# Product-key expert block: two token blocks by gathered rows and two by plain float32 products, in place of one and three

## The reference, cut to what matters

```python
q = (hf @ w_query).reshape(T, PEER_HEADS, 2, PEER_HALF)
s = jnp.einsum('thpd,pkd->thpk', q, sub_keys).astype(jnp.float32)
sv, si = lax.top_k(s, PEER_TOPK)
cand = (sv[:, :, 0, :, None] + sv[:, :, 1, None, :]).reshape(T, PEER_HEADS, PEER_TOPK * PEER_TOPK)
...
top_s, top_pos = lax.top_k(cand, PEER_TOPK)
idx = jnp.take_along_axis(cand_idx, top_pos, axis=-1)
g = jax.nn.softmax(top_s, axis=-1)
...
u = down[ib]
pre = jnp.einsum('td,thkd->thk', hb, u).astype(jnp.float32)
w = (gb * jax.nn.gelu(pre, approximate=False)).astype(hb.dtype)
return jnp.einsum('thk,thkd->td', w, up[ib])
```

## Time and profile before

| | before |
|---|---|
| median of 3 runs | 2176.43 us (2176.3 to 2180.94) |
| span of the profiled execution | 2176.0 us |
| TensorE busy | 1860.8 us (86%) |
| VectorE busy | 1542.3 us (71%) |
| ScalarE busy | 868.6 us (40%) |
| GpSimd busy | 740.9 us (34%) |
| bytes moved | 462.65 MB, 213 GB/s over the span |

### The profile page before, as it was taken

One profiled execution on the slowest core, in us unless ns is written; L12 is line 12 of the kernel. 1 busy time (PEld: TensorE's weight loads), 2 busy tenths in 40 slices (PEclk: granted clock), 3 DMA queues, 4 the chain that ended last, 5 costly groups with the idle time before them and its releaser, 6 DMA issues.

```text
span 2176.0 us, 27879 instructions
## 1 busy us (share of the span) xinstructions
PE 1860.8 (86%) x9219; PEld 1632.1 (75%) x9219; DVE 1542.3 (71%) x2326; ACT 868.6 (40%) x1434; POOL 740.9 (34%) x410
## 2 busy tenths in 40 slices
PE   2888999877397999979886888878869999999996
PEld 1676887844276889979886888878857888888884
DVE  5476445386756229967889787977857888888886
ACT  2232222355222244356633665355643333333332
POOL 0000000000000016677755777568763333333320
PEclk7898999987698999989987998979979999999998
DMA  7244442100231225578864887568889999999993
GB/s 266 96 144 150 177 153 95 40 1 1 96 107 58 97 72 171 168 241 278 289 217 151 286 285 262 176 215 291 279 310 352 354 359 357 352 352 360 347 360 142
DMA packets 177680, 462.65 MB, mean 213 GB/s; under 512 B 14624, under 2 KB 96800, under 8 KB 165152
## 3 DMA queue, kind: packets, MB, share of 16 engines
q1 hardware_dynamic: 117808, 272.99, 36.4%
q0 software_dynamic: 37872, 137.90, 18.6%
q10 hardware_dynamic: 21888, 50.34, 5.9%
HBM read 406.12 MB, written 55.05 MB: 212 GB/s over the span
## 4 chain that ended last, share of the span: by engine, by line
PE 53%; issue 15%; DVE 14%; POOL 11%; DVEq 3%; DMA 2%; ACT 2%; POOLq 0%; ACTq 0%; SPq 0%
PE bank L538 16%; PE bank L539 16%; PE bank L540 16%; POOL d_ring L1546 7%; POOL dlo L1523 4%; DVEq L1123 1%; DMA raw<-in_ada 1%; DMA d_ring<-in_down,idxd 1%; DVE att_max L1231 1%; DVE acc_ada L1077 1%; DVE onehot L1394 1%; PE bank L605 1%; DVE wlo L1096 1%; PE bank L593 1%; PE bank L724 1%
## 5 line engine op out<-in xcount | busy, mean ns | idle before, releaser
L1523 POOL TENSOR_TENSOR dlo<-draw,dhi 128x1024 fp32r<-128x1024 f32 x131 | 359.8, 2753 | 1002.4 <-ACT dhi L966 1002.0
L538 PE MATMUL bank<-r_hi,dhi 128*128 128x384 f32 x1024 | 360.2, 352 | 10.1 <-issue 5.5
L539 PE MATMUL bank<-r_lo,dhi 128*128 128x384 f32 x1024 | 355.4, 347 | 0.0
L540 PE MATMUL bank<-r_hi,dlo 128*128 128x384 f32 x1024 | 354.6, 346 | 0.0
L538 PE MATMUL bank<-uhi,w_hi 128*128 128x512 f32 x768 | 300.4, 391 | 17.4 <-issue 13.6
L539 PE MATMUL bank<-ulo,w_hi 128*128 128x512 f32 x768 | 299.7, 390 | 0.0
L540 PE MATMUL bank<-uhi,w_lo 128*128 128x512 f32 x768 | 299.7, 390 | 0.0
L1573 POOL DMA_INDIRECT u_ring<-in_up,idxc x128 | 170.6, 1333 | 276.7 <-DVE accum L1485 252.8
L1445 DVE CUSTOM_DVE_ANT_0 dot_junk<-d_ring,h2row 128x1024 f32<-128x1024 f32 x135 | 194.8, 1443 | 93.2 <-DMA d_ring<-in_down,idxd 83.8
L1038 ACT ACTIVATE uhi<-uraw 128x1024 fp32r<-128x1024 f32 x130 | 137.9, 1062 | 294.0 <-PE bank L540 181.6
L1096 DVE TENSOR_TENSOR wlo<-raw,whi 128x2048 fp32r<-128x2048 f32 x45 | 103.2, 2293 | 176.2 <-ACT whi L801 175.8
(11 more groups left out here) (218 smaller groups left out, 3599.0 us busy)
## 6 DMA issues: line engine op xcount, KB each, us to landing
draw<-in_downT SPq DMA_DIRECT2D x131, 512.0 KB
uraw<-in_up SPq DMA_DIRECT2D x130, 512.0 KB, 7.8
raw<-in_ada SPq DMA_DIRECT2D x24, 1024.0 KB, 4.9
ged<-ge ACTq DMA_DIRECT2D x128, 192.0 KB
gmat<-gstage ACTq DMA_DIRECT2D x24, 1024.0 KB, 7.2
gtile<-gmat SPq DMA_DIRECT2D x16, 1536.0 KB
gein<-ged SPq DMA_DIRECT2D x128, 192.0 KB, 7.2
raw<-in_w_query SPq DMA_DIRECT2D x8, 1024.0 KB, 4.9
```

What stands on the lines that cost most here:

```text
L538: pe.matmul(dst, lhi, rhi, start=first, stop=False)
L539: pe.matmul(dst, lhi, rlo, start=False, stop=False)
L540: return pe.matmul(dst, llo, rhi, start=False, stop=last)
L1523: pool.tensor_tensor(dlo[slot][:, :, :].rearrange("p a b -> p (a b)"), draw[:, slot, :], dhi[:, slot].rearrange("p a b -> p (a b)").bitcas ...
```

## The change

- Two blocks (0 and 1) are gathered, two (2 and 3, `DT` = 256 tokens) are dense. 256 gathers of `down` pass a ring of 4 buffers, 256 of `up` a ring of 8, of which four are the same and four lie over `h2T`.
- The dense products are plain float32, with no split: 8 products of 256 columns a tile of `down`, 4 products of 512 columns a tile of `up`. Tiles stream through 4 buffers. No `dhi`, `dlo`, `uhi`, `ulo`, `w_hi`, `w_lo`.
- The GELU results of all 128 tiles stay in SBUF (`wmat`, 128 KB a partition). After the last `down` tile a loop of 64 groups of four tokens builds one-hots (8 small VectorE instructions), multiplies them on TensorE (4 products), and multiplies the result into `wmat` in place (one VectorE instruction, 128x128x4, with a step of 1 KB between groups of 4 numbers in `wmat` and of 512 B between numbers in PSUM). Only then does the `up` half begin. `ged` and `gmat` are gone.
- `route` keeps, of the 256 pair sums, the 72 that can be among the top 16, and turns positions back by a short chain of small instructions (`unpair`). The dot products stand between its instructions (`dots`), one or two at a time, for blocks 1 to 3; 42 follow after the softmax, the other 88 after the 64 groups.
- The token-major copy of the block's vectors (`h2tok`) and the gate row move into the query stage.

The core of the diff:

```diff
-DTB = 3
-DT = DTB * P
+GB = 2
+DB = TB - GB
+DT = DB * P
 ET = 128
+SLOT0 = 18
+RING = 4
+URING = 8
+PAIRS = 72
...
+            for n in range(2 * ET):
+                if n >= RING:
+                    sp.wait_ge(tile_used, n - RING + 1)
+                src = downT[n] if n < ET else up[(n - ET) * P:(n - ET + 1) * P, :]
+                sp.dma_start(stream[:, n % RING, :], src).then_inc(stream_in[n % RING], 16)
...
-                for k in range(KT):
-                    last = mm3(bank[:, 6 + j % 2, 0:DT], dhi[:, slot, k, :], dlo[slot][:, k, :],
-                               r1_hi[:, k, 0:DT], r1_lo[:, k, 0:DT], k == 0, k == KT - 1)
...
+                for k in range(KT):
+                    last = pe.matmul(bank[:, 4 + i % 2, 0:DT], stream[:, i % RING, k * P:(k + 1) * P],
+                                     h2T[:, k, GB * P:S], start=(k == 0), stop=(k == KT - 1))
+                last.then_inc(tile_used, 1)
+
+            for q in range(DT // 4):
+                par = q % 2
+                pe.wait_ge(oh_ready, q + 1)
+                if q >= 2:
+                    pe.wait_ge(w_ready, q - 1)
+                else:
+                    pe.wait_ge(pickTs_ready, DB)
+                for n in range(4):
+                    last = pe.matmul(bank[:, 6 + par, n * P:(n + 1) * P], h2T[:, 4 * par + n, 0:P],
+                                     h2T[:, 4 * par + n, P:2 * P], start=True, stop=True)
+                last.then_inc(gmm, 1)
+
+            pe.wait_ge(w_ready, DT // 4)
...
+            for i in range(ET):
+                stream_tile(ET + i)
+                for tb in range(DB):
+                    for half in range(2):
+                        last = pe.matmul(bank[:, 2 * tb + half, :], wmat[:, wslot(i), tb * P:(tb + 1) * P],
+                                         stream[:, (ET + i) % RING, half * S:(half + 1) * S],
+                                         start=(i == 0), stop=(i == ET - 1))
+                last.then_inc(tile_used, 1)
...
+            for i in range(ET):
+                if i == EXP_AT:
+                    for n in range(TB):
+                        exponentials(n)
...
+                if 70 <= i < 70 + 8 * TB and i % 8 == 6:
+                    act.wait_ge(logit_ready, (i - 70) // 8 + 1)
+                if i == 102:
+                    act.wait_ge(pick_ready, DB)
+                act.wait_ge(tile_used, i + 1)
+                act.activation(wmat[:, wslot(i), :], bank[:, 4 + i % 2, 0:DT], ACT.Gelu).then_inc(ge_ready, 1)
...
+            def dots(count, upto=GB * P):
+
+                for g in range(done[0], min(done[0] + count, upto)):
+                    b, k = g // P, g % P
+                    dve.wait_ge(ring_in[g % RING], 16 * (g // RING + 1))
+                    dve.tensor_tensor_reduce(out=ring[g % RING][:, :], in0=ring[g % RING][:, :],
+                                             in1=h2row[:, b, :], scale=1.0, scalar=0.0, op0=ALU.mult,
+                                             op1=ALU.add, accum_out=pre[:, b, k:k + 1]).then_inc(dot_done, 1)
+                    done[0] = g + 1
...
+            def pairs():
+
+                one, two = top_v[:, :, 0, :], top_v[:, :, 1, :]
+                for a0, rows_, width, at_ in ((0, 1, 16, 0), (1, 3, 8, 16), (4, 4, 4, 40), (8, 8, 2, 56)):
+                    shape = [P, PH, rows_, width]
...
+            for n in range(TB):
+                for g in range(4):
+                    wait_emptied(dve, "score", 4 * n + g)
+                route(n, 1 if n else 0)
...
+            dots(P, P)
             dve.drain()
...
+            dots(DOTS_FIRST)
+
+            def one_hots(q):
...
+                for n in range(4):
+                    t = t0 + n
+                    dve.tensor_scalar(h2T[:, 4 * par + n, 0:P], iota, ijT[:, b, 1, t:t + 1], None, ALU.is_equal)
+                    last = dve.tensor_scalar(h2T[:, 4 * par + n, P:2 * P], iota_w, ijT[:, b, 0, t:t + 1],
+                                             gT[:, b, t:t + 1], ALU.is_equal, ALU.mult)
+                last.then_inc(oh_ready, 1)
+
+            def weigh(q):
+
+                dve.wait_ge(gmm, q + 1)
+                if q == 0:
+                    dve.wait_ge(ge_ready, ET)
+                w = wmat[:, :, 4 * q:4 * q + 4]
+                dve.tensor_tensor(w, bank[:, 6 + q % 2, :].rearrange("p (t i) -> p i t", t=4), w, ALU.mult)\
+                   .then_inc(w_ready, 1)
+
+            one_hots(0)
+            for q in range(DT // 4):
+                if q + 1 < DT // 4:
+                    one_hots(q + 1)
+                weigh(q)
+
+            dve.memset(accum[:, :, :], 0.0)
+            dots(GB * P)
...
+            for g in range(GB * P):
+                b, k, slot = g // P, g % P, g % URING
+                dve.wait_ge(ring_in[slot], 16 * ((GB * P // RING if slot < RING else 0) + g // URING + 1))
+                dve.scalar_tensor_tensor(accum[:, b, :], ring[slot][:, :], share[:, b, k:k + 1], accum[:, b, :],
+                                         ALU.mult, ALU.add).then_inc(sum_done, 1)
+                dve.drain()
...
+            for g in range(GB * P):
+                b, k = g // P, g % P
+                if k == 0:
+                    pool.wait_ge(idx_ready, b + 1)
+                if g >= RING:
+                    pool.wait_ge(dot_done, g - RING + 1)
+                gather(down, b, k, g % RING)
+            for g in range(GB * P):
+                b, k, slot = g // P, g % P, g % URING
+                if g >= URING:
+                    pool.wait_ge(sum_done, g - URING + 1)
+                elif slot < RING:
+                    pool.wait_ge(dot_done, GB * P - RING + slot + 1)
+                else:
+                    pool.wait_ge(w_ready, DT // 4)
+                gather(up, b, k, slot)
```

More of the change, by code:

```diff
@@ L95 @@
 RAW_SLOTS = 3
-def after_batch(b):
-    first = DNA + b * DNB * BT // P
-    return list(range(first, DNA + (b + 1) * DNB * BT // P))
-def rows_of_batch(b):
-    return list(range(3 * b - 3, 3 * b)) if b else []
 def tile_plan():
@@ L114, in tile_plan @@
             tiles += [("x1tok", n, "act") for n in range(8)]
+        if (s, c) == ("query", 4):
+            tiles += [("h2tok", n, "act") for n in range(2 * GB)]
+            tiles += [("gaterow", n, "dve") for n in range(2)]
         if s == "pool":
@@ L121, in tile_plan @@
             tiles += [(s, 2 * c + n, who) for n in range(2)]
-    tiles += [("h2tok", n, "dve") for n in range(2)]
-    tiles += [("gaterow", n, "dve") for n in range(2)]
     tiles += [("score", n, "act") for n in range(16)]
@@ L136, in emptied, with wslot, layer @@
     return who, sum(1 for t in TILES[:n + 1] if t[2] == who)
-def layer(nc, consts, chans, rows, xT_d, pos_d, subk_d, ada_d, wdram, downT, down, up, gmat, ged, x1d, gated, out):
+def wslot(i):
+    return (i + SLOT0) % ET
+def layer(nc, consts, chans, rows, xT_d, pos_d, subk_d, ada_d, wdram, downT, down, up, x1d, gated, out):
     f32, f32r = mybir.dt.float32, mybir.dt.float32r
@@ L396, in layer @@
[L396 to L409 removed]
+        w_ready = sem("w_ready")
@@ L661, in _ @@
                     t = tokens_first(t, x1T, range(8))
+                if stage == "query" and c == 4:
+                    pe.wait_ge(h2_ready, 8)
+                    t = tokens_first(t, h2T, range(2 * GB))
+                    for m in range(2):
+                        free_bank(t)
+                        pe.matmul(bank[:, t % 4, :], ones[:, :], acc_ada[:, 1, m * S:(m + 1) * S],
+                                  start=True, stop=True).then_inc(tile_ready, 1)
+                        t += 1
                 if c == 0:
@@ L782, in _, with stream_tile, pick_transpose @@
-            for b in range(2 * DTB):
-                last = pe.matmul(bank[:, b, :], zeros[:, 0:P], zeros[:, :], start=False, stop=True)
-            last.then_inc(psum_done, 1)
+            def stream_tile(n):
+                pe.wait_ge(stream_in[n % RING], 16 * (n // RING + 1))
+            def pick_transpose(b):
+                pe.wait_ge(pick_ready, b + 1)
+                for x in range(3):
+                    last = pe.transpose(bank[:, 6 + b, x * P:(x + 1) * P], picked[:, b, x, :], ident)
+                last.then_inc(pickT_ready, 1)
@@ L938, in _ @@
                 elif stage == "query":
+                    if c == 4:
+                        for k in range(2 * GB):
+                            act.activation(h2row[:, k // 2, (k % 2) * S:(k % 2 + 1) * S],
+                                           tile("h2tok", k), ACT.Copy).then_inc(act_emptied, 1)
                     for m in range(2):
@@ L1381, in route @@
[L1381 removed]
+                pairs()
                 top16([best[:, h] for h in range(PH)], [best_at[:, h] for h in range(PH)],
[L1383 to L1387 removed]
```

644 lines of the change are left out of this document (170 added, 474 removed).

## The result

The changed kernel takes **2069.83 us** (median of 4 runs, 2060.29 to 2072.81), the kernel before 2178.47 (median of 4, 2176.3 to 2180.94). The ratio is **0.9491, 95% interval 0.9467 to 0.9516**: 5.1% faster. The forecast was 2102 with a range of 2025 to 2185.

The account below looks back on a forecast made before the run. It took the first half as bound by hand-overs between engines, the second by TensorE and DMA together. Until the groups 1258, 64 groups 166, `up` half 656, tail 22: 2102 us, range 2025 to 2185.

Parts of the forecast that it names:

- a chain of hand-overs: First half of the kernel before: no engine full, engines hand work to each other, 800 us for three blocks.
- part (a): Start of the `up` half: 84 left dot products at the ring's 2.35 us beside tile loads, 197 us.
- I take 1.3: Dot products with rows ready: 1.3 us each once the drain goes, 164 us for the 126 in the routings.
- D: Rival: first half does not shrink, ring stalls stop dense tiles; 40 us late gives 2130; chance 0.52 together with the forecast.
- I take 1.2: 64 groups: VectorE's product into `wmat`, with a transposed walk of PSUM, costs 1.2 us of a group's 2.6.
- I take 1.4: 64 groups: VectorE's eight small instructions cost 1.4 us a group, between bounds of 1.1 and 2.3.
- part (b): `up` half: the other 67 tile loads go with TensorE in 230 us; 109 gathers beside them, 2.11 us each.
- part (c): End of the `up` half: 147 gathers alone at 1.5 us each, 221 us.
- I take 1.5: Gathers alone in the `up` half: GpSimd's issue and the time between issues set 1.5 us a gather.
- A: Rival: DMA at its 402 GB/s ceiling (613 us) and cheap groups of 2.1 us (134): 2027 us; chance 0.18.
- B: Rival: GpSimd issues slowly beside the sums, 1.6 + 0.3 us a gather, +58 us: 2160; chance 0.15.
- C: Rival: one gather after another, about 2.3 us each, 589 us for 256 `up` gathers: 2240; chance 0.15.

Follow-up runs that it names:

- the last run: Kernel before the change, without the gathered `down` rows and their dot products in its first half: 2058.64 us, 118 less.
- the last two edits: Changed kernel with the 88 left dot products among the groups, and with ScalarE making half of the one-hots: 2038.75 and 2047.17 us alone, 1992.49 together.

## Why the prediction was right, and where it was off

**The bound of the first half.** The forecast called it a chain of hand-overs. By the last run that holds for 120 of 800 us; in the others TensorE is nearly always busy. An estimate from its records at full clock: 531 us of split products, 86 of one-hot products, and 183 of waits and of time at the low clock. Now it is 443 us of plain products and nothing else. So the half lost 88 us of products, the 86 of one-hots (moved behind it, into the groups), and the 183. The 88 are what is left of a block taken away: split, a block costs TensorE 531 / 3 = 177 us, plain it costs 442.5 / 2 = 221, a quarter more. The plain product saves the splits on ScalarE and GpSimd, not time on TensorE. How much of the 109 us is due to it, and how much to the second gathered block, was not measured: no run has split products in two blocks or plain ones in three. The number for the new product, 0.22 us a record, did not depend on that reading and came out at 442.5 for 450.

**Routing and the ring.** One routing 46.5, measured 47.3 (794.9 to 842.2); softmax 1159, measured 1160.2; a dot behind them 2.35, measured 2.22 and, in part (a), 2.26. The ring's round of 9.4 us for a dot product held at 9.0. That the softmax comes out to a microsecond is in part luck. With its row ready a dot follows the one before in 1.15 us (1160.23 and 1161.37), not in "I take 1.3", which is some 20 us less for 126 of them; against that VectorE waited 23 us for rows instead of 15, and the first scores came 4 us later. What the forecast missed is how near the edge it stood: it took D for an accident of 40 us, and one buffer less costs 110.

**The groups.** The terms of the sum that were mis-sized are "I take 1.2" for the product and "I take 1.4" for the small ones. From start to start they took 0.60 and 1.80, 2.40 together, and 2.44 with the loop's start and end. The errors had opposite signs, so 2.6 became 2.44: the step came out near its forecast by luck. The row for the product should have been the contiguous VectorE product of 0.684; the strided `gstage` row on ScalarE did not carry over. The Trainium skill (SBUF — State Buffer, the note on cachelines) has non-contiguous PSUM reads slow matmuls. It speaks of matmuls alone, and for this VectorE read with a step of 512 bytes the trace shows no slowing, 0.682 against 0.684. In some other runs the record of the product is longer, up to a median of 0.84 with a ring of three, but the period of a group is 2.40 to 2.41 there too.

**That nothing covers the groups** was right, and half of them took half of it. The forecast saw DMA idle there and did not ask what could be moved into it; the last two edits did, for 77 us.

**The `up` half.** Part (a) came out at 199 for 197 by two errors that cancel: 126 + 42 of 256 leave 88 dots and not the 84 of the forecast, and a dot took 2.26 us and not 2.35. In part (b) the price held: 120 rows from 1608.6 to 1861, when TensorE ended, are 2.10 us each, for 2.11. The step that was mis-sized is part (c), and with it its mechanism: the forecast let GpSimd's issue set the pace ("I take 1.5") and looked for sums that wait on gathers. Measured are 1.38 us, and VectorE's sums do not wait; with their drains they are the bound. 147 x 0.12 is just the 17 us. The issues on GpSimd (us, start to start 1.38), and its source line from 1620 to 1850, where sums and tiles run together:

```profile
1899.60 1.07 POOL L1322 DMA_INDIRECT ring<-in_up,idx  x1 [0.30 <-issue]
1900.98 1.07 POOL L1322 DMA_INDIRECT ring<-in_up,idx  x1 [0.30 <-issue]
...
L1322 POOL DMA_INDIRECT ring<-in_up,idx x112: 932/939/1917, 1619.5 to 1849.3; - x112
```

**The rivals.** A had cheap groups (2.1, measured 2.44) and the full ceiling; the kernel came 43 us above it and 32 below the forecast. B fell: the issue beside sums has a median of 0.94 us while tiles come, the same as beside the dots, and 1.07 where the sums stand back to back, not 1.6. The Trainium skill (SBUF — State Buffer, on the shared port pair) has a VectorE instruction with two SBUF inputs contend with a GpSimd instruction that reads SBUF, which the forecast applied to the issue; the same section takes it that writing descriptors needs the pair's write side, and that such an instruction therefore does not hold them up. The trace agrees with the latter for the 0.94. Whether the 1.07 is a small contention is not shown. The issues there keep the very step of the sums, 1.07 + 0.30 = 1.37, and GpSimd waits for no buffer, so it has hardly more slack than VectorE; what would bound the rows if the sums were quicker was not tried. C fell: landings follow each other in 1.4 us. D did not happen, and is the one that lay closest.

## What to carry to other kernels

A step that one engine does alone while the DMA engines idle, next to a stretch in which they are full, is worth more than its own length: move transfers that are due anyway, with their consumers, into it, and take instructions off the engine that holds it. Each edit alone ran into the next bound (VectorE's time, ScalarE's time); together they gave 77 us where apart they gave 54. And read a ring by the rate beside it: with 345 of a possible 409 GB/s another buffer was worth 110 us, from 384 to 409 it was worth 5. Most of the 110 is not the rate itself but a neighbour that it stopped (73 us before the groups, where late picks held TensorE), so look also at who waits for the consumer of the ring. And read busy shares with the waits: at the end the DMA engines are at 0.98 to 1.00 and VectorE at 46 of 50, and it is VectorE that sets the pace.

## What was not expected of the hardware

- A VectorE product that reads PSUM with a step of 512 bytes and writes 16-byte pieces takes 0.682 us, the same as a contiguous one (0.684).
- A plain float32 product costs TensorE more than the same product in three fast parts: 221 us for a block of 128 tokens against 177.
- A gathered row's time round its buffer changes only from 7.6 to 10.1 us while the DMA share goes from 0.83 to 1.03; both simple readings of it, fixed or pure queueing, gave wrong forecasts here (+150, and +10 to +30, for a measured +110).
- Tiles and rows together reach 409 GB/s. Rows alone stay at 369 to 379, but there VectorE's sums (one in 1.38 us, 380 GB/s) are the bound; with a DMA share of 0.98 to 1.00 the share alone does not show that.
- In the run without `up` tiles, TensorE issued one 512-column record every 2.80 us from 1702 on, with no wait that the profile shows, after 290 us at full pace beside the same gathered rows. It ended with the last gather. Not explained.
- TensorE's granted clock was 0.66 in the groups, a mean of its two levels, and 0.50, that is 1.2 GHz throughout, once dots stood among them (it was busy 25 of 50 us); its work stayed hidden under VectorE's both times.
